# Attention scores of the first block: three rounded products of split queries and keys for one float32 product

## The chip, the cores and the metric

The program runs on one NeuronCore of a Trainium2 chip; the other cores are idle. The metric is the device time in microseconds (us) from the start to the end of one execution, and lower is better. Engines are named as in the profile: PE is TensorE's matrix multiplication, PEld its loading of the stationary operand (which can overlap PE), DVE is VectorE, ACT ScalarE, POOL GpSimd, SP the engine that issues DMAs here.

## What is computed

The reference runs two blocks on 512 tokens of width 1024. Only a part of the first block is touched, the differential attention of each of its two layers:

```python
qf = q.astype(f32).reshape(B, n_blk, Q_BLOCK, 2 * H, DIFF_DIM) * (DIFF_DIM ** -0.5)
...
s = jnp.einsum("bqmd,bkmd->bmqk", q_blk, kf)
dist = jnp.abs(qpos[:, None] - kpos[None, :]).astype(f32)
p = jax.nn.softmax(s - slopes[:, None, None] * dist, axis=-1)
p = p.reshape(B, H, 2, Q_BLOCK, S)
a = p[:, :, 0] - lam * p[:, :, 1]
return jnp.einsum("bhqk,bkhe->bqhe", a, vf)
```

H is 6 heads, each with two score maps m = 0 and 1 of width DIFF_DIM = 32. A block of queries is 128 tokens, and S is 512. The projections, a 31-tap depthwise convolution (computed beside the attention), the delta net, the MLP and the whole second block stay as they are.

## The kernel before

The first block is a loop of two turns (one for each layer); both turns run the same code, so every cost in the attention counts twice. Within a turn, each stage is a `phase` that starts and ends with a barrier of all engines: norm, projections, `diff_attention`, `delta_net`, norms and output projection, MLP. Inside a phase each engine follows its own list in the order in which the code is written, and waits on semaphores by hand-set counts.

`diff_attention` works through 24 units (j, t, h): j is one of three pairs of heads (a tile of 128 channels of q and k), t one of four blocks of 128 queries, h the head in the pair. A unit has two score maps, m = 0 and 1, in two PSUM banks of the four that `score_bank` hands out in turn. The two maps of a unit take their 32 channels from neighbouring lanes of the tile (lanes 0 to 31 and 32 to 63 for h = 0, 64 to 95 and 96 to 127 for h = 1).

- PE: after `scored(0)` and `scored(1)`, turn n is `scored(n + 2)`, `transposed(n)`, `apply(n - 1)` and, in every second turn, `turn_rows`. `scored` is the float32 product q times k for each m (L800, 32 rows of contraction, 512 columns), then one float32r product for each m that adds the distance term (L806). `transposed` turns the exponentials (L817), `apply` multiplies them with the values (L832, 16 instructions of 65 columns). `scored(n + 2)` waits until both exponentials of unit n are made, because it writes into their banks:

```python
if n >= 2:
    pe.wait_ge(exped, 2 * n - 2)
if (t, h) == (0, 0):
    pe.wait_ge(q_scaled, j + 1)
```

- ACT, unit n: `exponent(n)` (L742, two), `first_part(n - 2)` (L749), `take_rows` in every second unit from 5 on (L755), then the convolution's products `scale_taps` (L763), two after an even unit and three after an odd one. `exponent(n)` waits for the row minima of its unit. The queries are scaled in place by `scale_query` (L734), the first at the start and two more ahead of the units.
- DVE, unit n: `top(n)` (row minima, L865), `second_part(n - 3)` (L886), `take_turned(n - 1)` (L872), `invert_sums(n - 2)` (L877), which waits for the end of `apply(n - 2)` on PE. Ahead of the units DVE makes lambda, slopes, the rounded distances (L907), the values, the gated input of the convolution (L913) and its first tap (L917).
- POOL adds each scaled tap to y (L729, 60 in a turn).

Elsewhere (`linear`, L491 to L493) the kernel already makes a product of two float32 matrices as three float32r products: high times high, high times low, low times high, where high is the rounded value and low the rounded rest. `parts_of` allocates such a pair of tensors.

## Time and profile before

| | |
|---|---|
| median of 3 runs | 4620.15 us (4614.26 to 4620.54) |
| profiled execution, its own time | 4617.3 us |
| its span, first to last instruction | 4615.5 us |
| mean granted clock of TensorE | 0.891 of full speed |
| busy share of the span: PE, PEld, DVE, ACT, POOL | 88%, 73%, 36%, 29%, 4% |
| attention phase, first turn of the loop | from 187.5 to 307.6 us of the span |
| attention phase, second turn | from 1303.6 to 1423.7 us |

The busy share is an average over stages with different limits; what the attention waits for is read from its own stretches. A clock of 1.00 is 2.4 GHz, one of 0.50 is 1.2 GHz. The end of a matmul's record is modelled and includes latency: successive records overlap, so what one costs in a stream is the distance from its start to the next start, not its length.

### The profile page before, as it was taken

What the parts mean: (1) busy time and instruction counts of PE and PEld (TensorE: products, weight loads), DVE (VectorE), ACT (ScalarE), POOL (GpSimd) and SP (SyncE); (2) the same over time, 40 slices, a digit from 0 to 9 for tenths busy, and PEclk for the clock granted to TensorE, in tenths of its full rate; (3) what the DMA queues carried; (4) which work ended last, traced back from release to release, by engine and by line L of the source; (5) the groups of instructions that cost most, each with busy time, mean ns of one, the idle gap of its engine ahead of it and who ended that gap; (6) DMA issues with size and microseconds to landing.
All of it is one profiled execution on the core that took longest, in us unless ns stands there. A gap on an engine that the chain in (4) does not pass through costs nothing. (4 is left out here: it accounts for less than half of the span.)

```text
span 4615.5 us, 55382 instructions
## 1 busy us (share of the span) xinstructions
PE 4050.1 (88%) x21416; PEld 3361.9 (73%) x21416; DVE 1641.0 (36%) x2889; ACT 1327.6 (29%) x2306; POOL 194.7 (4%) x160
## 2 busy tenths in 40 slices
PE   7997888997998887999786777999878879999998
PEld 5777776775777775787465655787655569999998
DVE  2365435233246434423335434332245421111112
ACT  2464523231256433322132222222223311111111
POOL 0141000000033000000000000000000000000000
PEclk9997779998998878999897878999986689999999
DMA  3100012221200001222110001222220014545443
GB/s 116 41 1 1 0 37 82 86 96 45 99 5 1 0 0 55 91 91 91 55 59 1 0 18 64 80 99 76 89 91 0 18 49 182 191 161 189 167 152 130
DMA packets 51453, 324.51 MB, mean 70 GB/s; under 512 B 6528, under 2 KB 7424, under 8 KB 20352
## 3 DMA queue, kind: packets, MB, share of 16 engines
q1 hardware_dynamic: 51328, 322.85, 19.4%
q8 instruction: 78, 1.28, 0.1%
q14 instruction: 47, 0.39, 0.0%
HBM read 319.68 MB, written 2.10 MB: 70 GB/s over the span
## 5 line engine op out<-in xcount | busy, mean ns | idle before, releaser
L491 PE MATMUL bank<-high 128*128 128x512 f32 x2480 | 980.7, 395 | 116.0 <-DVE low L585 81.1
L492 PE MATMUL bank<-low,high 128*128 128x512 f32 x2480 | 976.4, 394 | 0.0
L493 PE MATMUL bank<-high,low 128*128 128x512 f32 x2480 | 975.4, 393 | 0.0
L491 PEld LDWEIGHTS bank<-high 128*128 128x128 f32 x2480 | 473.0, 191 | 224.2 <-issue 67.3
L492 PEld LDWEIGHTS bank<-low,high 128*128 128x128 f32 x2480 | 473.6, 191 | 98.5
L493 PEld LDWEIGHTS bank<-high,low 128*128 128x128 f32 x2480 | 472.7, 191 | 99.6
L549 DVE TENSOR_TENSOR low<-weight_ring,high 128x2048 fp32r<-128x2048 f32 (+1 forms) x144 | 319.2, 2218 | 553.1 <-ACT high L506 553.1
L2860 PE MATMUL bank<-chosen,glu_ring 128*128 128x176 f32 x2816 | 422.0, 313 | 0.0
L2860 PEld LDWEIGHTS bank<-chosen,glu_ring 128*128 128x128 f32 x2816 | 420.1, 190 | 0.0
L506 ACT ACTIVATE high<-weight_ring 128x2048 fp32r<-128x2048 f32 (+1 forms) x144 | 266.6, 1852 | 269.1 <-PE bank L493 230.2
L2871 PE MATMUL bank<-hidden,down_ring 128*128 128x176 f32 x1408 | 211.3, 313 | 0.0
L2871 PEld LDWEIGHTS bank<-hidden,down_ring 128*128 128x128 f32 x1408 | 210.4, 190 | 0.0
L1395 DVE TENSOR_TENSOR joint<-bank,level_masks 128x512 f32<-128x512 f32 x224 | 152.3, 689 | 129.4 <-PE bank L1410 129.4
L729 POOL TENSOR_TENSOR y<-y,scaled 128x512 f32<-128x512 f32 x120 | 149.6, 1274 | 1023.3 <-ACT scaled L763 1023.3
L2949 DVE TENSOR_TENSOR hidden<-silu,bank 128x176 f32<-128x176 f32 x88 | 29.7, 338 | 390.7 <-ACT silu L2917 390.7
L557 DVE TENSOR_TENSOR gated<-gated,bank 128x512 f32<-128x512 f32 x86 | 58.9, 685 | 287.5 <-ACT gated L513 158.2
L2917 ACT ACTIVATE silu<-bank 128x176 f32<-128x176 f32 x88 | 27.9, 317 | 445.5 <-PE bank L2860 445.5
L1417 PE MATMUL bank<-weight_ring,joint 128*128 128x128 f32 x1152 | 152.5, 278 | 0.0
L610 ACT ACTIVATE u<-bank 128x512 f32 (+1 forms) x84 | 50.3, 598 | 335.3 <-PE bank L493 335.3
L1410 PE MATMUL bank<-const_cols,weight_ring 128*128 128x128 f32 x672 | 108.3, 294 | 41.3 <-PEq L172 41.3
L1417 PEld LDWEIGHTS bank<-weight_ring,joint 128*128 128x128 f32 x1152 | 142.0, 195 | 0.0
L279 PE MATMUL bank<-squares,const_cols 128*128 128x512 f32 x144 | 82.6, 738 | 66.4 <-DVE squares L288 66.4
(465 smaller groups left out, 4972.9 us busy)
## 6 DMA issues: line engine op xcount, KB each, us to landing
glu_ring<-in_w_expert SPq DMA_DIRECT2D x88, 1024.0 KB, 4.8
weight_ring<-in_w_ff SPq DMA_DIRECT2D x64, 1024.0 KB, 5.2
down_ring<-in_w_expert_down SPq DMA_DIRECT2D x64, 704.0 KB, 5.1
weight_ring<-in_w_in SPq DMA_DIRECT2D x22, 1024.0 KB, 4.9
weight_ring<-in_w_ffe SPq DMA_DIRECT2D x22, 1024.0 KB, 4.8
weight_ring<-in_w_downe SPq DMA_DIRECT2D x16, 704.0 KB, 4.0
weight_ring<-in_w_ino SPq DMA_DIRECT2D x11, 1024.0 KB, 4.8
weight_ring<-in_w_ine SPq DMA_DIRECT2D x9, 1024.0 KB, 4.8
```

The source lines that it names most:

```text
L279: last = nc.tensor.matmul(total[:, :], CONST(mem.const, "ones"), squares[:, k, :], start=(k == 0), stop=(k == KD - 1))
L491: nc.tensor.matmul(mem.bank[b][:, :], whole, high[:, k, :], start=(k == 0), stop=False)
L492: nc.tensor.matmul(mem.bank[b][:, :], whole, low[:, k, :], start=False, stop=False)
L493: last = nc.tensor.matmul(mem.bank[b][:, :], rest, high[:, k, :], start=False, stop=(k == kt - 1))
L506: nc.scalar.activation(w_high[:, s, :], mem.ring[:, s, 0:size], ACT.Copy).then_inc(high_ready[s], 1)
L549: nc.vector.tensor_tensor(w_low[:, s, :], mem.ring[:, s, 0:size], w_high[:, s, :], ALU.subtract).then_inc(low_ready[s], 1)
L729: nc.gpsimd.tensor_tensor(y[:, c, :], y[:, c, :], scaled[:, n % CONV_SLOTS, :], ALU.add).then_inc(added, 1)
L1395: nc.vector.tensor_tensor(chunks(joint[:, n, :]), chunks(mem.bank[2 * n + 1][:, :]), mask, ALU.mult) \
L1410: last = nc.tensor.transpose(mem.bank[2 * n + 1][:, c], matrix[:, n, c], ident)
L1417: last = nc.tensor.matmul(mem.bank[2 * n][:, c], joint[:, n, c], matrix[:, n, c], start=True, stop=True)
L2860: last = nc.tensor.matmul(two(low[s])[:, half, :], glu_ring[:, s, at:at + P], chosen[:, k, :], start=(k == 0), stop=(k == KD - 1))
L2871: last = nc.tensor.matmul(two(high[m // 2])[:, m % 2, :], down_ring[:, s, k * P:(k + 1) * P], hidden[:, k, :], start=(k == 0), stop=(k == ...
```

## The change

The queries and keys of a pair of heads are split into a rounded value and a rounded rest, and the score product of each m becomes three float32r products (high q with high k, high q with low k, low q with high k), taken in turns over the two maps. ACT writes the two high parts (`round_pair`, which now also scales the queries), DVE the two rests (`rest_of_pair`). The first pair is split at the start of the phase, the next ones inside the loop, five or six units before they are used. To make room, `sig`, `probs`, `raw_dist`, `turned` and `scaled` move to memory that is free in this phase (the branch tensor `mem.h` and the weight ring); what is written and read there is the same.

```diff
-    with buffers(nc, padded=[P, CONV_T, SEQ + CONV_WIDTH - 1], sig=[P, CONV_T, SEQ], scaled=[P, CONV_SLOTS, SEQ],
-                 raw_dist=[P, DIST_COLS], prod=[P, 2, DIFF_DIM], dots=[P, 4], coef=[P, 1],
-                 values=[P, 2, TT, DIFF_HEADS, wide], probs=[P, 4, SEQ], turned=[P, 4, SEQ],
+    sig, probs = mem.h[:, 0:CONV_T, :], mem.h[:, 4:8, :]
+    raw_dist = mem.h[:, 2:4, :].rearrange("p k s -> p (k s)")[:, 0:DIST_COLS]
+    turned, scaled = [mem.ring[:, i, :].rearrange("p (n s) -> p n s", s=SEQ) for i in range(2)]
...
+            parts_of(nc, PAIRS1) as q_parts, parts_of(nc, PAIRS1) as k_parts, \
...
         @block.scalar
         def _(act):
-            def scale_query(j):
-                nc.scalar.activation(u[:, U_DQ + j, :], u[:, U_DQ + j, :], ACT.Copy, scale=-DIFF_DIM ** -0.5) \
-                    .then_inc(q_scaled, 1)
+            def round_pair(j):
+                nc.scalar.activation(q_parts[0][:, j, :], u[:, U_DQ + j, :], ACT.Copy, scale=-DIFF_DIM ** -0.5) \
+                    .then_inc(qk_high, 1)
+                nc.scalar.activation(k_parts[0][:, j, :], u[:, U_DK + j, :], ACT.Copy).then_inc(qk_high, 1)
...
-            scale_query(0)
+            round_pair(0)
...
-            for j in range(1, PAIRS1):
-                scale_query(j)
             act.wait_ge(padded_ready, CONV_T)
             for n in range(n_units):
+                if units[n][1:] == (TT - 2, 0) and units[n][0] + 1 < PAIRS1:
+                    round_pair(units[n][0] + 1)
                 exponent(n)
...
                 if (t, h) == (0, 0):
-                    pe.wait_ge(q_scaled, j + 1)
-                for m in range(2):
-                    lanes = slice(DIFF_DIM * (2 * h + m), DIFF_DIM * (2 * h + m + 1))
-                    nc.tensor.matmul(score_bank(2 * n + m)[:, :], u[lanes, U_DQ + j, t * P:(t + 1) * P],
-                                     u[lanes, U_DK + j, :], start=True, stop=False)
+                    pe.wait_ge(qk_split, 2 * j + 2)
+                for q_part, k_part in ((0, 0), (0, 1), (1, 0)):
+                    for m in range(2):
+                        lanes = slice(DIFF_DIM * (2 * h + m), DIFF_DIM * (2 * h + m + 1))
+                        nc.tensor.matmul(score_bank(2 * n + m)[:, :], q_parts[q_part][lanes, j, t * P:(t + 1) * P],
+                                         k_parts[k_part][lanes, j, :], start=(q_part == k_part), stop=False)
...
         def _(dve):
             steps = Steps(dve, dve_steps)
 
+            def rest_of_pair(j):
+                dve.wait_ge(qk_high, 2 * j + 1)
+                nc.vector.scalar_tensor_tensor(out=q_parts[1][:, j, :], in0=u[:, U_DQ + j, :], scalar=-DIFF_DIM ** -0.5,
+                                               in1=q_parts[0][:, j, :], op0=ALU.mult, op1=ALU.subtract) \
+                    .then_inc(qk_split, 1)
+                dve.wait_ge(qk_high, 2 * j + 2)
+                nc.vector.tensor_tensor(k_parts[1][:, j, :], u[:, U_DK + j, :], k_parts[0][:, j, :], ALU.subtract) \
+                    .then_inc(qk_split, 1)
...
+            rest_of_pair(0)
             for m in range(2):
                 steps.did(nc.vector.tensor_tensor(prod[:, m, :], lam_rows[:, 2 * m * DIFF_DIM:(2 * m + 1) * DIFF_DIM],
...
             for n in range(n_units):
+                if units[n][1:] == (TT - 2, 1) and units[n][0] + 1 < PAIRS1:
+                    rest_of_pair(units[n][0] + 1)
                 top(n)
```

In PE's list, units 0 and 1 and turn 0 of the attention stand as follows before (a row stands for a float32 product once, though it is two instructions on the engine):

```order
L800 MATMUL bank<-u 128x512 x2
L806 MATMUL bank<-dist,slopes 128x512 x2
L800 MATMUL bank<-u 128x512 x2
L806 MATMUL bank<-dist,slopes 128x512 x2
L800 MATMUL bank<-u 128x512 x2
L806 MATMUL bank<-dist,slopes 128x512 x2
L817 MATMUL bank<-const_cols,probs 128x128 x8
```

and now, with the score product at L805 and the distance term at L811 (`h_branch` is the new place of `probs`), unit 1 and turn 0:

```order
L805 MATMUL bank<-high 128x512 x2
L805 MATMUL bank<-low,high 128x512 x2
L805 MATMUL bank<-high,low 128x512 x2
L811 MATMUL bank<-dist,slopes 128x512 x2
L805 MATMUL bank<-high 128x512 x2
L805 MATMUL bank<-low,high 128x512 x2
L805 MATMUL bank<-high,low 128x512 x2
L811 MATMUL bank<-dist,slopes 128x512 x2
L822 MATMUL bank<-const_cols,h_branch 128x128 x8
```

A unit's score is six one-instruction products in place of two that are two instructions each; nothing else on PE moved.

In ACT's list, this stands around `exponent(4)` before (the exponentials of units 2, 3 and 4, with the taps behind each):

```order
L742 ACTIVATE probs<-bank,tops 128x512 x2
L749 ACTIVATE part<-bank,inv 128x64
L763 ACTIVATE scaled<-padded,vec 128x512 x2
L742 ACTIVATE probs<-bank,tops 128x512 x2
L749 ACTIVATE part<-bank,inv 128x64
L763 ACTIVATE scaled<-padded,vec 128x512 x3
L742 ACTIVATE probs<-bank,tops 128x512 x2
```

and now, from the exponentials of unit 3 on:

```order
L746 ACTIVATE h_branch<-bank,tops 128x512 x2
L753 ACTIVATE part<-bank,inv 128x64
L767 ACTIVATE weight_ring<-padded,vec 128x512 x3
L737 ACTIVATE high<-u 128x512
L739 ACTIVATE high<-u 128x512
L746 ACTIVATE h_branch<-bank,tops 128x512 x2
```

The two roundings stand between the taps of unit 3 and the exponentials of unit 4; the same is so ahead of unit 12.

In DVE's list, `top(5)` followed the reciprocal of unit 2 at once; now the two rests stand between them, and likewise ahead of `top(13)`:

```order
L891 RECIPROCAL inv<-bank 128x2
L869 SCALAR_TENSOR_TENSOR low<-u,high 128x512
L873 TENSOR_TENSOR low<-u,high 128x512
L879 TENSOR_REDUCE tops<-bank 128x1 x2
L900 SCALAR_TENSOR_TENSOR rows<-bank,inv,part 128x64
```

## Rows read from the trace of the kernel before

**Rows 1.** Windows: length, busy us of PE, PEld, DVE, ACT, POOL; PEclk; DMA.
```profile
188.65:209.13 20.48, 16.47 (x47) 8.42 (x43) 11.04 (x25) 12.81 (x19) 6.17 (x5) 0.50 0.06 22
209.13:308.10 98.97, 96.57 (x687) 76.30 (x686) 61.98 (x134) 67.39 (x133) 68.61 (x55) 1.00 0.00 1
...
245.00:260.00 15.00, 15.00 (x101) 11.13 (x101) 10.04 (x22) 10.19 (x21) 9.95 (x9) 1.00 0.01 2
```
**Rows 2.** Waits from 215 to 300 us: who waited for whom, total, times, longest.
```profile
ACT part L749 <- DVE inv L877: 26.2, 20, 1.6
DVE inv L877 <- PE bank L832: 15.5, 19, 0.8
```
**Rows 3.** Timeline of one steady turn on PE: start, length, engine, line.
```profile
227.72 1.13 PE L800 MATMUL bank<-u 32*128 32x512 f32 x4
...
228.78 0.30 PEld L806 LDWEIGHTS bank<-dist,slopes 128*128 128x128 f32 x2 [0.76 <-issue]
...
232.16 1.13 PE L800 MATMUL bank<-u 32*128 32x512 f32 x4
```
**Rows 4.** Narrow windows in that turn: its four score instructions, and their loads.
```profile
227.72 0.70 PE L800 MATMUL bank<-u 32*128 32x512 f32 x2
...
228.26 0.59 PE L800 MATMUL bank<-u 32*128 32x512 f32 x2
...
227.83 0.19 PEld L800 LDWEIGHTS bank<-u 32*128 32x128 f32 x2
```
**Rows 5.** Timeline of float32r products in a stream, at full and at half clock.
```profile
150.12 0.39 PE L492 MATMUL bank<-low,high 128*128 128x512 f32 x1
150.35 0.39 PE L493 MATMUL bank<-high,low 128*128 128x512 f32 x1
...
66.57 0.63 PE L492 MATMUL bank<-low,high 128*128 128x512 f32 x1
66.99 0.63 PE L493 MATMUL bank<-high,low 128*128 128x512 f32 x1
```
**Rows 6.** By line: the query scaling; then timeline at the phase's start.
```profile
L734 ACT ACTIVATE u<-u x6: 612/614/629, 187.5 to 1310.6; 128x512 f32<-128x512 f32 x6
...
192.16 0.16 DVE L902 TENSOR_TENSOR coef<-dots 128x1 f32<-128x1 f32 x1 [2.75 <-ACT dots L770]
194.03 1.13 ACT L734 ACTIVATE u<-u 128x512 f32<-128x512 f32 x2
196.96 1.26 ACT L742 ACTIVATE probs<-bank,tops 128x512 f32<-128x512 f32 x2 [1.80 <-DVE tops L865]
198.28 2.08 PE L800 MATMUL bank<-u 32*128 32x512 f32 x4 [0.79 <-ACT probs L742]
```
**Rows 7.** Timeline where ACT makes the exponentials of units 4 and 12.
```profile
217.00 1.25 ACT L742 ACTIVATE probs<-bank,tops 128x512 f32<-128x512 f32 x2
218.96 0.70 PE L800 MATMUL bank<-u 32*128 32x512 f32 x2
...
252.08 1.26 ACT L742 ACTIVATE probs<-bank,tops 128x512 f32<-128x512 f32 x2
254.01 1.13 PE L800 MATMUL bank<-u 32*128 32x512 f32 x4
```
**Rows 8.** Timeline of DVE, ACT and POOL around unit 13.
```profile
254.21 1.26 DVE L865 TENSOR_REDUCE tops<-bank 128x1 f32<-128x512 f32 x2
255.76 1.25 ACT L742 ACTIVATE probs<-bank,tops 128x512 f32<-128x512 f32 x2
251.04 3.74 POOL L729 TENSOR_TENSOR y<-y,scaled 128x512 f32<-128x512 f32 x3 [1.98 <-ACT scaled L763]
258.45 1.13 PE L800 MATMUL bank<-u 32*128 32x512 f32 x4
```
**Rows 9.** DVE operations with two SBUF inputs, by line: shortest, median, longest ns.
```profile
L585 DVE TENSOR_TENSOR low<-h_branch,high x8: 682/683/691, 63.7 to 67.9; 128x512 fp32r<-128x512 f32 x8
L298 DVE SCALAR_TENSOR_TENSOR h_branch<-x_res,vec,scale x8: 746/746/752, 30.0 to 34.6; 128x512 f32<-128x512 f32 x8
```

More of the change, by code:

```diff
@@ L691, in diff_attention @@
     taps = [(i, c) for i in range(1, CONV_WIDTH) for c in range(CONV_T)]
-    with buffers(nc, padded=[P, CONV_T, SEQ + CONV_WIDTH - 1], sig=[P, CONV_T, SEQ], scaled=[P, CONV_SLOTS, SEQ],
-                 raw_dist=[P, DIST_COLS], prod=[P, 2, DIFF_DIM], dots=[P, 4], coef=[P, 1],
-                 values=[P, 2, TT, DIFF_HEADS, wide], probs=[P, 4, SEQ], turned=[P, 4, SEQ],
+    sig, probs = mem.h[:, 0:CONV_T, :], mem.h[:, 4:8, :]
+    raw_dist = mem.h[:, 2:4, :].rearrange("p k s -> p (k s)")[:, 0:DIST_COLS]
+    turned, scaled = [mem.ring[:, i, :].rearrange("p (n s) -> p n s", s=SEQ) for i in range(2)]
+    with buffers(nc, padded=[P, CONV_T, SEQ + CONV_WIDTH - 1], prod=[P, 2, DIFF_DIM], dots=[P, 4], coef=[P, 1],
+                 values=[P, 2, TT, DIFF_HEADS, wide],
                  tops=[P, 2 * n_units], inv=[P, n_units, 2], part=[P, 2, HEAD], rows=[P, 2, P]) as (
-            padded, sig, scaled, raw_dist, prod, dots, coef, values, probs, turned, tops, inv, part, rows), \
+            padded, prod, dots, coef, values, tops, inv, part, rows), \
+            parts_of(nc, PAIRS1) as q_parts, parts_of(nc, PAIRS1) as k_parts, \
             nc.sbuf_tensor(f"dist_{nc.next_id()}", [P, DIST_COLS], F32R) as dist, \
             nc.sbuf_tensor(f"slopes_{nc.next_id()}", [P, DIFF_HEADS, P], F32R) as slopes, phase(
-            nc, "loaded", "q_scaled", "gate_ready", "dots_ready", "exps_ready", "coef_ready", "bias_ready",
+            nc, "loaded", "qk_high", "qk_split", "gate_ready", "dots_ready", "exps_ready", "coef_ready", "bias_ready",
             "values_ready", "values_scaled", "padded_ready", "conv_begun", "scaled_ready", "added", "score", "topped",
@@ L702, in diff_attention @@
             "rows_taken", "dve_steps") as (
-            block, loaded, q_scaled, gate_ready, dots_ready, exps_ready, coef_ready, bias_ready,
+            block, loaded, qk_high, qk_split, gate_ready, dots_ready, exps_ready, coef_ready, bias_ready,
             values_ready, values_scaled, padded_ready, conv_begun, scaled_ready, added, score, topped,
```

## The prediction, on record before the changed kernel ran

> **What bounds the kernel now.** I read the page for the stages, then the windows of the attention phase, its waits, and its timeline. The page says that PE is busy 88% of the span, which tells nothing of this phase; the windows do: from 245 to 260 us PE is busy for all 15.00 us, while DVE has 10.04, ACT 10.19 and POOL 9.95 [rows 1]. The waits have only one sort of entry: the reciprocal on DVE waits for PE, and ACT's `part` waits for that reciprocal [rows 2]. Nobody makes PE wait in the steady turns. A turn lasts 4.44 us (227.72 to 232.16, the two score starts [rows 3]). So what PE saves in a turn is saved in the phase, as long as ACT and DVE keep up. The exception is the start: PE's third score, at 198.28, waits for the first exponentials on ACT, and these for DVE's row minima [rows 6]. The granted clock is 0.50 from 188.65 to 209.13 us and 1.00 behind it [rows 1].
>
> **What the score costs now.** From the first score instruction to the distance term is 228.78 - 227.72 = 1.06 us for both maps [rows 3]. The narrow windows show how: two instructions start at 227.72, two at 228.26, and the second pair's loads at 227.83, while the first pair streams [rows 4]. The two maps use different lanes and run side by side. The first pair takes 0.54 us, the second 0.52 to the distance term. I read 0.43 of each as two streams of 512 columns (a float32r instruction, one such stream, has starts 0.427 apart at half clock, 66.57 to 66.99 [rows 5], so a stream at full clock is 0.213), and the other 0.11 and 0.09 as fixed: the first load, which nothing covers (the second record, 0.59, is shorter than the first, 0.70, by just that), and the change from 32-row to 128-row products, ahead of which PEld is idle [rows 3, 4].
>
> **What it will cost.** Six float32r instructions, three pairs in a row. In a stream such products start 0.23 apart (150.12, 150.35; 0.227 over several [rows 5]). No row shows one with 32 rows. If they pair as float32 does: 3 x 0.227 = 0.68 for 0.853 of streams, and both fixed parts stay. That saves 0.17 us in a turn. Bounds: 3 x 0.213 = 0.64 (saves 0.21) if the 0.014 of overhead hides under the partner, and 6 x 0.227 = 1.36 (loses 0.51) if nothing pairs. I take 0.17, since row groups of 32 lanes and loads are the same as in [rows 4], and only the number type differs. At half clock the saving is 1.71 - 3 x 0.427 = 0.43.
>
> How often: units 0 and 1 lie ahead of the wait at 198.28 and save nothing. Units 2 and 3 are scored at half clock: 0.86. Units 4 to 23 are 20 at full clock: 3.5 us.
>
> **The start.** ACT has one more operation ahead of the sigmoids. Two such copies in a row take 1.13, a single one 0.61 [rows 6], so one adds 0.52. DVE begins with two rests that it must wait for, but it stands idle 2.75 us ahead of L902 anyway, waiting for ACT [rows 6]; two operations of such sizes take 0.75 and 0.68 [rows 9], and with the wait for the high parts they end about 2.1 us later than DVE began before. That fits into the idle time; without this cover they would cost those 2.1 instead of 0.52. Lambda, distances, the first minima and so PE's third score come 0.52 late, at half clock. The two queries that ACT no longer scales at 194.03 were covered by its wait of 1.80 [rows 6] and give nothing. Of 0.86 saved at half clock, 0.86 - 0.52 = 0.34 is left, which is worth half once the clock has risen: 0.15 us.
>
> **The roundings inside the loop.** `round_pair` stands ahead of `exponent(4)` and `exponent(12)`, behind three taps. Before, those exponentials run from 217.00 to 218.25 and from 252.08 to 253.34, and PE, which needs them for the score two units on, starts at 218.96 and 254.01 [rows 7]. Slack: 0.71 and 0.67, of which 0.06 is what the semaphore takes (198.22, the end of the first exponentials, to 198.28 [rows 6]). Two copies add 2 x 0.52 = 1.04, and PE wants the result 0.17 earlier than before. PE stalls 1.04 - (0.65 - 0.17) = 0.56, and 1.04 - (0.61 - 0.17) = 0.60: 1.16 us in a phase. Behind it in ACT's list stand `part` and the taps, which POOL waits for; POOL has a third of its time free.
>
> `rest_of_pair` delays DVE ahead of `top(5)` and `top(13)` by 0.66 + 0.60, some 1.3 us (the distance of such operations in a row: 30.0 to 34.6 and 63.7 to 67.9 us over seven steps [rows 9]). For unit 13, minima start at 254.21, the exponentials at 255.76, held by ACT's own taps, and end at 257.01; PE needs them at 258.45 [rows 8]. With 1.3 more the minima end at 256.8, the last exponential at 257.5. Slack is left, and the rests cost nothing. `take_turned` on DVE starts later by less than PE's stall. The rests themselves are wanted two turns on.
>
> **The sum.** One phase: -0.15 - 3.5 + 1.16 = -2.5 us; two turns of the loop: -5.0. Moved buffers: nothing, the one DMA is the same. Of the profiled time of 4617.3 us that leaves 4612.3. The median of the runs lies 2.9 higher than the profiled run, 4620.15, so I expect **4615.2 us**, 0.11% less.
>
> **A rule on shared ports.** POOL's additions, 1.25 us each, run while the rests would: three from 251.04 to 254.78 [rows 8]. No DVE operation in this phase has two SBUF inputs beside POOL, so no row has its price. The Trainium skill (SBUF — State Buffer, Who interferes with whom) says that a DVE instruction with two SBUF inputs and a GpSimd instruction that reads SBUF block each other for a whole instruction. What blocking as a mechanism would cost here follows from [rows 8]: the first rest waits for 254.78, 0.57 late, the second for one more addition, 1.25. The minima then end at 258.6, the exponentials at 259.3, against PE's need at 258.45 + 0.6 - 0.17 = 258.9: up to 0.4 us more stall at each of four places, 1.7 in all, or 4616.9. I give this a chance of 0.3, inside the main case below, which it hardly moves. By that rule, rests in the loop would have records of over 1 us.
>
> **Rivals.**
> - *Loads no longer hide* (0.10). A stream is now 0.213 long, not 0.43, and must cover the next load to the same lanes, 0.11. For: each load of the first pair is exposed. Against: the second pair's load starts at 227.83, inside the first pair's stream on the same lanes [rows 4]. If each pair shows its load: 3 x (0.213 + 0.107) = 0.96 + 0.09 = 1.05, no saving in a turn. Nothing is saved, the late start costs 0.26 (0.52 at half clock) and the stalls are 2 x 0.17 shorter, 0.8: 2 x 1.06 = +2, or 4622. The same skill (TensorE: Matmul & The Clock Gate, Part 3, The mechanism) says that a load overlaps a matmul only when the row group differs, which would be this case; the 227.83 load contradicts it, so the chance is small.
> - *No pairing of float32r: slower* (0.13). PE runs them one behind the other, from one map's to the other's. Each unit loses 0.51 at full clock (20 units, 10.2 us) and 0.85 at half clock (1.7 for two, with the late start 2.2, worth 1.1). ACT's stalls vanish, since its slack grows to 1.16. Sum 2 x 11.3 = +22.6: 4643. It decides as soon as fewer than about half of the pairs overlap. For: no row with 32 rows in float32r. Against: the maps and banks are what pairs float32.
> - *Clock* (0.04). Less streaming on PE could keep the half clock longer at the phase's start: each us costs half, 20 us more in both phases would be +20. Against: PE is as gapless as before from 198.8 us on.
> - *Better than the sum* (0.10). Overhead hides (0.21 in a turn) and the copies squeeze into ACT's slack: 2 x (4.3 + 0.15) = -8.9, with luck in the later, clock-dependent stages beyond -9: 4610.
>
> **How the numbers follow.** The main case has 0.63, from -9 to +0.5 us. A difference under 0.2% (9.2 us) is about what a measurement can't tell from none; the three runs before spread over 6.3 us. Same: main, hidden loads, and part of the better case: 0.71. Slower: no pairing and clock: 0.17. Faster: the rest of the better case and the low end of the main one, with luck in later stages: 0.12. The range for eight in ten leaves out the case without pairing and half of the outermost: 4608 to 4625.
>
> **What would show it.** L805 with 288 records, in three pairs of starts 0.23 apart, and 0.88 us from first score start to distance term (1.06 before). The turn of 4.44 becomes 4.27. PE waiting for ACT's exponentials twice in a phase, near 219.4 and 254, by 0.6. The first distance term at 193.6, the third score at 198.8. I am wrong if the six records start one after the other, if the stalls are over 1 us, or if the clock rises later than some 21 us after its fall.

## The result: 5.7 us longer, outside the range

| | before | after |
|---|---|---|
| median of 22 runs each, us | 4620.34 | 4626.03 |
| all runs, us | 4606.82 to 4633.55 | 4621.54 to 4637.98 |
| ratio of the two, 95% interval | | 1.0017, 1.0009 to 1.0025 |
| profiled execution, span, us | 4615.5 | 4624.1 |

Forecast were 4615.2 us and a range of 4608 to 4625. That is 0.12%, under the 0.2% that the prediction took for what a measurement can't tell from none, but it is 5.7 us more where 5.0 less was forecast. (The ratio here and below isn't the quotient of the two medians; where the two disagree, the text says so.)

**Inside the attention nearly every step came as forecast.** By line, the new score instructions (columns: shortest, median, longest ns; first and last start), and the remainders on DVE:
```profile
L805 PE MATMUL bank<-high x96: 489/494/792, 188.3 to 1416.0; 32*128 32x512 f32 x96
L805 PE MATMUL bank<-low,high x96: 382/392/627, 188.9 to 1416.4; 32*128 32x512 f32 x96
L805 PE MATMUL bank<-high,low x96: 383/392/627, 189.3 to 1416.6; 32*128 32x512 f32 x96
...
L869 DVE SCALAR_TENSOR_TENSOR low<-u,high x6: 693/1240/1291, 187.0 to 1377.6; 128x512 fp32r<-128x512 f32 x6
...
L873 DVE TENSOR_TENSOR low<-u,high x6: 677/679/685, 187.6 to 1378.8; 128x512 fp32r<-128x512 f32 x6
```
PE's timeline where the scores of units 5 and 6 are made (start, us, line; answers to [rows 3, 7]):
```profile
212.87 0.50 PE L805 MATMUL bank<-high 32*128 32x512 f32 x2
213.21 0.39 PE L805 MATMUL bank<-low,high 32*128 32x512 f32 x2
213.44 0.40 PE L805 MATMUL bank<-high,low 32*128 32x512 f32 x2
213.76 0.73 PE L811 MATMUL bank<-dist,slopes 128*128 128x512 f32 x2
214.33 1.04 PE L822 MATMUL bank<-const_cols,h_branch 128*128 128x128 f32 x8
215.21 1.90 PE L837 MATMUL bank<-values,weight_ring 128*128 128x65 f32 x16
217.58 0.50 PE L805 MATMUL bank<-high 32*128 32x512 f32 x2 [0.47 <-ACT h_branch L746]
```
Two maps still run side by side (x2 in one row), a score takes 213.76 - 212.87 = 0.89 us (1.06 in [rows 3]), and the turn that ends at 217.58 holds a stall that is new (the 0.47 in brackets). The waits from 205 to 300 us count two of them (total, times, longest; [rows 2] had none):
```profile
PEld bank L805 <- ACT h_branch L746: 1.3, 2, 0.7
PE bank L805 <- ACT h_branch L746: 1.0, 2, 0.5
```
DVE, POOL and ACT beside that stall:
```profile
217.23 1.25 DVE L869 SCALAR_TENSOR_TENSOR low<-u,high 128x512 fp32r<-128x512 f32 x1
218.40 0.68 DVE L873 TENSOR_TENSOR low<-u,high 128x512 fp32r<-128x512 f32 x1
...
214.19 3.74 POOL L732 TENSOR_TENSOR y<-y,weight_ring 128x512 f32<-128x512 f32 x3 [1.67 <-ACT weight_ring L767]
218.42 3.03 POOL L732 TENSOR_TENSOR y<-y,weight_ring 128x512 f32<-128x512 f32 x2 [0.49 <-ACT weight_ring L767]
...
215.24 0.62 ACT L737 ACTIVATE high<-u 128x512 fp32r<-128x512 f32 x1
215.76 0.62 ACT L739 ACTIVATE high<-u 128x512 fp32r<-128x512 f32 x1
216.28 1.25 ACT L746 ACTIVATE h_branch<-bank,tops 128x512 f32<-128x512 f32 x2
```
The two roundings push the exponentials of unit 4 to 216.28, and PE gets them 0.5 us late.

**What the attention saved, the stage behind it gave back.** Windows of before: the attention, `delta_inputs` behind it, and the three `delta_scan` of the first pass (length; busy us of PE, PEld, DVE, ACT, POOL; PEclk):
```profile
187.50:308.40 120.90, 113.48 (x732) 85.02 (x732) 74.08 (x164) 81.31 (x153) 74.79 (x60) 0.91 0.02 5
308.40:347.80 39.40, 30.98 (x216) 30.79 (x216) 24.04 (x49) 24.60 (x44) 0.00 (x0) 0.74 0.00 1
...
406.90:434.40 27.50, 23.10 (x176) 17.47 (x176) 4.87 (x23) 4.39 (x12) 0.00 (x0) 0.88 0.00 1
492.50:526.90 34.40, 30.25 (x176) 21.32 (x176) 4.87 (x23) 4.39 (x12) 0.00 (x0) 0.60 0.00 0
584.90:616.20 31.30, 27.50 (x176) 18.57 (x176) 4.87 (x23) 4.39 (x12) 0.00 (x0) 0.66 0.00 0
```
The same of after:
```profile
186.30:304.70 118.40, 108.99 (x780) 90.15 (x780) 78.70 (x170) 82.99 (x156) 75.90 (x60) 0.91 0.02 5
304.70:346.70 42.00, 33.57 (x216) 33.38 (x216) 24.04 (x49) 24.71 (x44) 0.00 (x0) 0.72 0.00 1
...
405.50:440.00 34.50, 30.28 (x176) 21.33 (x176) 4.87 (x23) 4.42 (x13) 0.00 (x0) 0.60 0.01 1
497.90:529.60 31.70, 27.51 (x176) 18.57 (x176) 4.88 (x23) 4.40 (x13) 0.00 (x0) 0.66 0.00 0
588.70:624.80 36.10, 32.26 (x176) 23.07 (x176) 4.87 (x23) 4.39 (x12) 0.00 (x0) 0.56 0.00 0
```
The attention is 2.5 us shorter, as forecast, and `delta_inputs` 2.6 us longer with the same 216 products: its PE is busy 2.6 us longer at a lower mean clock. From the phase's first ACT operation to the first of `delta_prepare`, the stage after `delta_inputs`, it is 160.27 us before and 160.38 after (second pass 160.33 and 160.79). The scans, in which the kernels' code is the same, differ by +7.0, -2.7 and +4.8, and each time the longer one has the lower clock. In these two profiles, the whole difference of 8.6 us is already there when the second pass starts (1303.6 and 1312.2 us), and the three scans alone make 9.1.

The two stages ahead of the scans can be taken apart further. Stretches around `delta_inputs` of before, then of after:
```profile
308.12:328.60 20.48, 13.87 (x65) 13.88 (x66) 17.24 (x35) 13.21 (x23) 0.00 (x0) 0.50 0.00 1
328.60:347.80 19.20, 17.11 (x153) 16.92 (x152) 6.80 (x14) 11.39 (x21) 0.00 (x0) 1.00 0.00 1
...
306.43:326.91 20.48, 15.88 (x74) 15.88 (x75) 15.63 (x30) 12.24 (x23) 0.00 (x0) 0.50 0.00 1
330.32:333.74 3.42, 3.42 (x18) 3.42 (x18) 2.10 (x6) 1.84 (x3) 0.00 (x0) 0.50 0.01 2
```
Before, the clock falls 0.3 us ahead of the stage, stays at 1.2 GHz for 20.5 us and is at 2.4 GHz from there to the stage's end. After, it falls 1.7 us into the stage, so that more of the products lie under the 20.5 us, and it falls once more later, for 3.4 us. (In the second pass of after it falls 1.5 us ahead of the stage, for 23.9 us, and again 25.8 us into it for 3.4.) In the first pass PE is busy at half clock for 13.87 us before and for 15.88 + 3.42 = 19.30 after. Work at half clock takes twice its time, so half of the difference, 2.7 us, is an estimate of the loss; measured are 2.6.

So two things had to be found out: whether the clock or the splitting makes `delta_inputs` longer, and where the scatter of some 20 us between executions comes from, in which 5 us must be seen.

### The profile page after: what moved, and what is told of

It is laid out like the page before. It is cut to its first block and busy times, and to the rows that moved or that the text cites. A ratio compares the mean times of both kernels' runs of the same rounds, so it can differ in the third digit from the quotient of the medians.

```text
span 4624.1 us, 55592 instructions
## 1 busy us (share of the span) xinstructions
PE 4055.5 (88%) x21512; PEld 3383.8 (73%) x21512; DVE 1650.3 (36%) x2901; ACT 1331.5 (29%) x2312; POOL 197.0 (4%) x160
## 5 line engine op out<-in xcount | busy, mean ns | idle before, releaser
L732 POOL TENSOR_TENSOR y<-y,weight_ring 128x512 f32<-128x512 f32 x120 | 151.8, 1291 | 1020.0 <-ACT weight_ring L767 1020.0
```

Source lines behind the costliest of these rows:

```text
L732: nc.gpsimd.tensor_tensor(y[:, c, :], y[:, c, :], scaled[:, n % CONV_SLOTS, :], ALU.add).then_inc(added, 1)
```

## The experiments

Theory A: TensorE's granted clock steps between 1.2 and 2.4 GHz, and what a stage takes depends on where a stretch at half clock lies on its products; an attention that ends sooner moves that stretch. Theory B, the rival: the splitting itself costs the stages behind it. All runs, with ratios to before on the same chip; the last two columns are read from the profiled execution, first pass / second pass: us from the phase's first ACT operation to the first product of `delta_inputs`, and to the first operation of `delta_prepare`.

| run | median us (lowest to highest, n) | ratio, 95% | to first product | to `delta_prepare` |
|---|---|---|---|---|
| before | | | 127.2 / 127.2 | 160.3 / 160.3 |
| after | 4626.0 (4621.5-4638.0, 22) | 1.0017, .0009-.0025 | 124.7 / 125.0 | 160.4 / 160.8 |
| e1, after, +10 pairs | 4631.9 (4619.9-4644.0, 5) | 1.0038, .0025-.0051 | 127.3 / 127.0 | 160.2 / 159.8 |
| e2, after, +5 pairs | 4641.5 (4623.0-4655.2, 6) | 1.0055, .0034-.0076 | 125.8 / 125.8 | 159.3 / 159.3 |
| e3, after, +15 pairs | 4634.3 (4629.7-4649.8, 6) | 1.0043, .0030-.0057 | 128.2 / 128.2 | 163.8 / 163.8 |
| e4, before, shortened | 4623.0 (4612.1-4639.4, 12) | 1.0017, .0004-.0029 | 124.7 / 124.7 | 160.6 / 160.6 |
| e5, after, filled | 4622.8 (4602.3-4639.4, 12) | 0.9994, 0.9978-1.0010 | 124.6 / 122.9 | 157.5 / 154.2 |
| e6, before, filled | 4611.9 (4601.3-4640.6, 12) | 0.9977, .9960-.9994 | 124.8 / 124.8 | 152.9 / 157.7 |
| e7, moved, filled | 4609.2 (4600.6-4625.7, 9) | 0.9967, .9952-.9981 | 121.9 / 121.9 | 150.0 / 150.0 |
| e8, moved, filled, scans | 4582.6 (4580.6-4586.9, 4) | 0.9909, .9894-.9924 | 121.9 / 121.9 | 153.2 / 153.3 |
| e9, before, scans | 4593.4 (4588.1-4604.4, 6) | 0.9938, .9924-.9952 | 126.9 / 127.3 | 159.8 / 160.4 |
| e10, after, scans | 4602.7 (4586.3-4604.6, 6) | 0.9946, .9930-.9962 | 125.1 / 124.6 | 160.8 / 160.2 |
| e11, before, filled, scans | 4587.8 (4585.9-4588.5, 5) | 0.9924, .9911-.9936 | 124.8 / 124.8 | 152.9 / 157.7 |
| e12, after, filled, scans | 4584.9 (4579.6-4585.5, 5) | 0.9917, .9904-.9929 | 122.9 / 122.9 | 154.2 / 154.2 |
| e13, moved, trimmed | 4580.2 (4572.5-4587.0, 5) | 0.9918, .9904-.9931 | 119.6 / 119.6 | 154.3 / 149.4 |
| e14, before, trimmed | 4575.0 (4573.9-4582.3, 5) | 0.9913, .9899-.9926 | 122.5 / 122.5 | 157.1 / 153.9 |
| e15, after, trimmed | 4576.9 (4572.1-4577.8, 4) | 0.9909, .9894-.9924 | 122.3 / 122.2 | 156.9 / 156.8 |
| e16, before, tail only | 4586.6 (4584.0-4599.8, 6) | 0.9928, .9911-.9945 | 127.6 / 127.7 | 160.6 / 160.7 |
| e17, after, tail only | 4580.7 (4577.3-4590.6, 6) | 0.9915, .9899-.9931 | 125.1 / 125.0 | 156.5 / 156.4 |
| e18, moved, tail only | 4579.7 (4572.9-4586.1, 6) | 0.9909, .9893-.9925 | 124.1 / 124.1 | 157.1 / 157.1 |

### 1. Length alone: e1 to e4

e1 to e3 add superfluous high-high pairs (their result is overwritten) to the changed kernel's last units (e1 one for n >= 14, e2 one for n >= 19, e3 e1's and one more for n >= 19):
```diff
-                for q_part, k_part in ((0, 0), (0, 1), (1, 0)):
+                extra = 1 if n >= 14 else 0
+                for p, (q_part, k_part) in enumerate(((0, 0),) * (extra + 1) + ((0, 1), (1, 0))):
...
-                                         k_parts[k_part][lanes, j, :], start=(q_part == k_part), stop=False)
+                                         k_parts[k_part][lanes, j, :], start=(q_part == k_part), stop=(p < extra))
```
e4 takes the kernel before and shortens it by as much as the change did, by leaving out the distance term of the second map from unit 13 on (its output is therefore not the reference's):
```diff
+                    alone = m == 1 and n >= 13
...
-                                     u[lanes, U_DK + j, :], start=True, stop=False)
+                                     u[lanes, U_DK + j, :], start=True, stop=alone)
...
+                    if m == 1 and n >= 13:
+                        continue
```
Expected of e1:

> The changed kernel with one superfluous pair of high-high products (overwritten by the next) in each of the units 14 to 23: 10 pairs of 0.23 us, so the attention is as long as in the kernel before (some 120 us) with PE busy. Theory A (what the attention saves is lost because the next stage, delta_inputs, meets the half-clock stretch at another place): delta_inputs falls back from 42.0 to about 39.4 us in both turns, and the time to that of before, ratio 1.000 +- 0.001, although 4.6 us of work were added. Theory B (the splitting itself costs somewhere, whatever its length): delta_inputs stays at 42.0 and the ratio is 1.0017 + 4.6/4620 = 1.0027.

Of e2:

> The same with 5 superfluous pairs in units 19 to 23: the attention is 1.1 us longer than in the changed kernel, 2.3 us in both turns. Theory B: ratio 1.0022. Theory A gives no straight line: delta_inputs somewhere between 39.4 and 42.5, and a ratio between 1.000 and 1.002, which must not be the mean of its neighbours.

Of e3:

> The same with 15 superfluous pairs: 3.4 us longer than the changed kernel, 6.8 us in both turns. Theory B: ratio 1.0032. Theory A: if the clock falls at the same place in the next stage as in the changed kernel, delta_inputs is 42.0 again and the ratio also about 1.003; if at the place of before, 39.4 and 1.001.

Of e4:

> The kernel before, with float32 scores and no splitting, but shorter: the distance term of the second score map is left out in units 13 to 23 (11 products of 0.23 us), so its result is not the reference's. Attention 117.6 us in place of 120.1. Theory A: delta_inputs grows from 39.4 to 42.0 here too, and the ratio is 1.000 to 1.002, not below 1, though 5 us of work are gone. Theory B: delta_inputs stays at 39.4 and the ratio is 1 - 5/4620 = 0.9989.

Windows of the attention and `delta_inputs` in e1:
```profile
186.90:307.80 120.90, 111.56 (x800) 92.26 (x800) 78.71 (x170) 82.88 (x156) 75.87 (x60) 0.91 0.02 5
307.80:347.10 39.30, 30.89 (x216) 30.70 (x216) 24.03 (x49) 24.59 (x43) 0.00 (x0) 0.75 0.01 1
```
The same in e2:
```profile
185.80:305.30 119.50, 109.42 (x790) 90.67 (x790) 78.73 (x170) 82.99 (x156) 75.97 (x60) 0.93 0.02 5
305.30:345.10 39.80, 31.34 (x216) 31.15 (x216) 24.04 (x49) 24.63 (x44) 0.00 (x0) 0.74 0.00 1
```
In e3:
```profile
186.20:308.10 121.90, 112.48 (x810) 92.94 (x810) 78.69 (x170) 82.92 (x156) 75.89 (x60) 0.92 0.02 5
308.10:350.10 42.00, 33.54 (x216) 33.35 (x216) 24.04 (x49) 24.75 (x44) 0.00 (x0) 0.72 0.01 1
```
In e4:
```profile
187.70:306.10 118.40, 110.92 (x721) 83.20 (x721) 74.10 (x164) 81.37 (x154) 74.85 (x60) 0.91 0.02 5
306.10:348.30 42.20, 33.83 (x216) 33.63 (x216) 24.04 (x49) 24.70 (x43) 0.00 (x0) 0.69 0.01 1
```
With the attention lengthened by 2.5 us and the splitting kept (e1), `delta_inputs` is back at 39.3; with the kernel before shortened by 2.5 us and no splitting (e4), it is 42.2, and the whole is as much longer as the changed kernel: 1.0017 in both. That refutes theory B for this stage. It is no straight line either: 42.0 at 118.4, 39.8 at 119.5, 39.3 at 120.9, 42.0 again at 121.9. The second stretch at half clock tells the two groups apart: after, e3, e4 and e10, whose stage takes 42 us, have one of 3.4 us some 25 us into it, in both passes; before, e1, e2 and e9, at 39 to 40 us, have none. But the totals don't follow: by the medians e1, e2 and e3 are 12.9, 22.5 and 15.3 us above before on the same chip. The ratio of e1 is over theory A's (1.000), and theory B's 1.0027 lies in its interval; that of e2 is over both (A up to 1.002, B 1.0022); e3's interval just reaches the 1.003 of both. So it is the stage's own length that speaks against theory B here, and e4, not these totals. The profiled execution of e1 is the fastest of its five (4619.9), so its trace can't show why the median is high. The spreads of 24 and 32 us of e1 and e2 pointed at the scans.

### 2. The clock held up: e5 to e8

e5 to e8 give PE products nobody reads where it waits:
```diff
+def fill(nc, mem, bank, count):
+    for _ in range(count):
+        nc.tensor.matmul(mem.bank[bank][:, 256:256 + P], CONST(mem.const, "ones"), CONST(mem.const, "ident"),
+                         start=True, stop=True)
...
+            fill(nc, mem, 5, 8)
             scored(0)
             scored(1)
+            fill(nc, mem, 5, 6)
...
+            fill(nc, mem, 3, 28)
             pe.wait_ge(g_ready, 1)
```
e7 and e8 also move the roundings apart (ACT; the remainders on DVE likewise), and e8 fills each `delta_scan`:
```diff
-                if units[n][1:] == (TT - 2, 0) and units[n][0] + 1 < PAIRS1:
-                    round_pair(units[n][0] + 1)
+                if units[n][1:] == (TT - 3, 0) and units[n][0] + 1 < PAIRS1:
+                    round_query(units[n][0] + 1)
+                if units[n][1:] == (TT - 2, 0) and units[n][0] + 1 < PAIRS1:
+                    round_key(units[n][0] + 1)
...
+            fill(nc, mem, 4, 8)
             pe.wait_ge(solved_taken, 4)
```

Expected of e5 to e8, in this order:

> The changed kernel with work on TensorE that nobody reads (ones times the identity, 128 x 128) where it waits around the attention: 8 products before the first scores, 10 before the first distance term, 6 after the second unit's scores, 6 ahead of each of the last row turns and 6 behind them, and 28 before the first product of delta_inputs. The output is unchanged. Theory A (what the attention saves is given back because TensorE's granted clock steps fall elsewhere in the stage behind it): with no stretch at half clock there, delta_inputs takes the same time as in the kernel before with the same filling, some 36 us or less in both, and this kernel is 4 to 6 us shorter than that one in the two turns taken together. Theory B (the splitting itself makes the following stage longer): delta_inputs stays 2.5 us longer than in the kernel before with the same filling, and their times agree within 2 us. If the clock falls all the same, neither is tested.

> The kernel before with the same filling on TensorE at the same places. The output is unchanged. Theory A: delta_inputs without a stretch at half clock, 36 us or less against 39.4, attention a little under its 120.9; in all 4605 to 4615 us. Theory B says nothing of this kernel by itself: it is what the changed kernel with filling is compared with, and by B the two agree within 2 us.

> The changed kernel with the same filling, and the two roundings of a pair on ScalarE apart, the queries' ahead of unit 2 (10) and the keys' ahead of unit 4 (12), with the two remainders on VectorE apart likewise. The output is unchanged. Forecast from the stalls of the changed kernel: each pair of roundings together (1.24 us) made the scores of units 6 and 14 0.53 and 0.60 us late; one alone (0.62 us) fits the slack of some 0.65 us that this leaves per turn, so both stalls go: the attention 1.0 to 1.2 us shorter than with filling alone, and 2 to 2.4 us off the whole if the clock stays up behind it (theory A); nothing off the whole if the following stages give it back.

> The one before it with 8 more superfluous products in each delta_scan, while TensorE waits for the copies of the solved values. The output is unchanged. Theory A in its wider form (the scatter of 20 us between executions is delta_scan of 27.6 or 34.5 us, by whether TensorE's clock falls some 13.6 us into it): most of the six scans of the first block's two passes take 27.6 us, and the whole is 10 to 30 us shorter with less scatter. If the scans stay at 31 to 34.5 us, the fall isn't due to that wait, and the time is that of the one before within 5 us.

The half-clock stretch of 20 us at the attention's start is gone in all four. In `delta_inputs` the clock fell all the same, for 13.7 and 10.2 us in e5's two passes and for 3.4 and 13.7 in e6's, so for that stage these runs test neither theory, as e5's expectation says for this case. Up to the first product of `delta_inputs` the change is then worth 124.8 - 122.9 = 1.9 us (e5's second pass; in the first the clock dropped once more), and apart from its stalls 2.9 (e7). The totals of e5 and e6 say the opposite, +11 us, with spreads of 37 and 39 us: that expectation was missed, and runs that scatter so can't carry it. e8 shows where most of the scatter comes from. Its three scans of the first pass:
```profile
397.60:425.90 28.30, 25.04 (x192) 19.41 (x192) 4.88 (x23) 4.39 (x12) 0.00 (x0) 0.86 0.01 2
483.60:508.70 25.10, 21.86 (x192) 16.43 (x192) 4.89 (x23) 4.41 (x13) 0.00 (x0) 0.96 0.00 0
567.60:598.70 31.10, 28.21 (x192) 22.35 (x192) 4.88 (x23) 4.40 (x13) 0.00 (x0) 0.78 0.00 0
```
Each has sixteen more records of PE, some of them on the path (28.3 against the 27.5 of before's best), and yet the median is 26.6 us under e7's and 46.5 under that of before, with a spread of 6 us (four runs) against e7's 25 (nine). The expectation had most scans at 27.6 us; instead they take 28.3, 25.1 and 31.1, and half-clock time is left in each. What the filling brought is that they are the same each time: in the profiles of all runs from e8 on, both passes have these three lengths to 0.4 us (e13's second pass in another order), while the same scans without it took anything from 24.0 to 38.0 us.

### 3. The change with calmer scans: e9 to e12

e9 is before and e10 after with the scans' filling alone, e11 and e12 have the filling of e5 as well. Expected of e9 to e12:

> The kernel before with 8 products that nobody reads (ones times the identity, 128 x 128) in each delta_scan, ahead of its wait for the copies of the solved values, and no other filling. The output is unchanged. Where the last run but one of this study found delta_scan to be the source of the scatter (the same 8 products, with other edits beside them, took the spread from 20 to 30 us down to 6 and the median down by 1.0%), this kernel has a spread of at most 12 us and lies at 4575 to 4600 us. It is the ruler for the next one.

> The changed kernel with the same 8 products in each delta_scan and no other filling. The output is unchanged. Theory A (what the attention saves is given back in delta_inputs by where the clock steps fall): attention 118.5 and delta_inputs 42 against 120.9 and 39.4, and a total within 2 us of that of the kernel before with the same products. The prediction's sum, had it been right for the whole kernel: 5 us less. Theory B (the splitting itself costs): 4 to 10 us more, as between the two kernels without the products.

> The kernel before with the products in delta_scan and with the filling around the attention (24 products at its start, 30 at its end, 28 before the first product of delta_inputs). The output is unchanged. The clock stays up in the attention, which ends some 4 us earlier than without filling, and its last products are some 2.7 us late behind too much filling; 3 to 12 us less in all than with the products in delta_scan alone. It is the ruler for the next one.

> The changed kernel with the products in delta_scan and the filling around the attention. The output is unchanged. Theory A: from the first operation of the attention to the first product of delta_inputs it is 1.9 us shorter per pass than the kernel before with the same filling (seen in profiles without the products in delta_scan: 122.8 against 124.8), and with the scatter gone the whole is shorter too, by 3 to 6 us for two passes, since no half-clock stretch behind the attention takes it back. Against the run with the roundings moved apart (4582.6) it is 1.5 to 3 us longer. Theory B: no shorter than the kernel before with the same filling.

e11 and e12 go as theory A says, at the low end: 2.9 us between the medians, and each of e12's five runs is under each of e11's on the same chip; 1.9 us a pass up to the first product. `delta_inputs` still isn't equal: in the first pass e11 reaches `delta_prepare` 1.3 us sooner than e12 (152.9 and 154.2), in the second 3.5 us later, as its clock fell for 3.4 and 13.7 us against 10.2 in both of e12's. Without the attention's filling, e9 and e10 reach `delta_prepare` level over the two passes (320.2 and 321.0 us together) and come out of the first block alike (`token_major`'s third start is at 2239.8 and 2239.3 us), so nothing of what the attention saved is left there. Yet e10's median is 9.3 above e9's where 2 were expected (by the ratios 0.08%, under 4 us), and their spreads, 16 and 18 us, are over the 12 that e9's expectation allowed. Of the 6 us between their profiles, 6.7 arise in `sparse_attention`, 1200 us on (222.2 and 228.9 us), which neither kernel fills. That the change makes that stage fall the bad way more often isn't shown.

### 4. Less filling, and a dip of the change's own: e13 to e15

As e8, e11 and e12, but 3, 3 and 2 products at the attention's end, 20 ahead of `delta_inputs`, and 3 in each `rwkv_scan`, a stage of the second block. Expected:

> The changed kernel with the roundings apart, the products in delta_scan, and the filling around the attention cut so that it no longer delays anything: 3, 3 and 2 products at the attention's end in place of 6, 6 and 6, and 20 in place of 28 ahead of delta_inputs; 3 more in each rwkv_scan. The output is unchanged. The first product of delta_inputs came 17.8 us after the attention's last exponential with the longer filling and 15.1 without; here 15.1 to 15.5 if the clock stays up, so up to 2.5 us per pass less. 4572 to 4582 us, and 4 to 8 us below the kernel before with the same additions.

> The kernel before with the same products in delta_scan, in rwkv_scan and around the attention. The output is unchanged. 4580 to 4588 us; from the first operation of the attention to the first product of delta_inputs 122 us (127.2 without any filling). It is the ruler for the other two.

> The changed kernel with the same products in delta_scan, in rwkv_scan and around the attention, the roundings where the change put them. The output is unchanged. Theory A: below the kernel before with the same additions by 1.9 us per pass in the attention, 2 to 5 us in all (2.9 between the medians of the pair with the longer filling), and 1.5 to 3 us above the run with the roundings apart.

The expected order didn't come: by the medians e15 is 1.9 above e14 and e13 5.1, while by the ratios e15 is a hair below e14 (0.9909 and 0.9913), so between those two nothing is decided; e14 is also 5 us faster than its expectation began. For e15 the trace shows a loss inside the attention. PE's timeline at the first stall:
```profile
212.48 0.50 PE L811 MATMUL bank<-high 32*128 32x512 f32 x2 [0.47 <-ACT h_branch L752]
...
213.37 1.07 PE L818 MATMUL bank<-dist,slopes 128*128 128x512 f32 x2
214.24 1.91 PE L829 MATMUL bank<-const_cols,h_branch 128*128 128x128 f32 x8
```
and the two windows behind it:
```profile
212.50:213.55 1.05, 1.05 (x7) 0.64 (x8) 1.05 (x2) 1.05 (x3) 0.55 (x2) 1.00 0.00 0
213.56:216.98 3.42, 3.42 (x16) 3.12 (x15) 3.18 (x6) 1.58 (x3) 2.77 (x2) 0.50 0.01 2
```
e14 at the same place:
```profile
213.00:217.00 4.00, 4.00 (x29) 3.11 (x30) 2.83 (x6) 2.69 (x5) 3.12 (x3) 1.00 0.01 2
```
PE came back from the stall that the roundings made at 212.48, was busy without a gap, and 1.1 us later its clock fell for 3.4 us: eight transposes took 1.91 us instead of 1.04. It did so in both passes, and not in e13, where the stall is gone: its score instructions no longer stand in its list of waits, and from the first to the 24th unit's exponentials it took 94.1 us against 96.7 in e15 and 97.5 in e14. e12 separates the dip from the stall: its attention is the same as e15's up to the last turns, has the same two stalls and no dip, and takes 95.1 us in both passes. So the dip cost 1.7 us, and the two stalls together 1.0 (e12 against e13). Such a dip is rare: the nine profiles with the roundings in pairs have 36 such stalls, and three of them have one, the two here and one in e5's first pass. All three began 1.1 us after PE had resumed, which ties them to the stall; all three are in kernels whose attention's start is filled. Why the other 33 had none isn't shown. e13's total is high all the same: three of its four `rwkv_scan` took the longer 22 us where e14 and e15 have one, and `sparse_attention` 228.9 against 222.4 in e14.

### 5. Only the stage behind: e16 to e18

As e14, e15 and e13 without the filling at the attention's start. Expected:

> The kernel before with the filling at the attention's end (3, 3, 2), 20 products ahead of delta_inputs, 8 in each delta_scan and 3 in each rwkv_scan, and none at the attention's start. The output is unchanged. The attention begins with its 20.5 us at half clock as in the kernel before; delta_inputs takes what it took with this filling, 36.4 us in the first pass. It is the ruler for the other two; 4580 to 4590 us.

> The changed kernel with the same filling. The output is unchanged. Theory A (only where the clock steps fall behind the attention takes back what it saved): the attention is shorter by 2.5 us per pass as without filling, delta_inputs the same in both kernels within 0.5 us in the first pass, so delta_prepare begins 2.0 us earlier relative to the end of the stage ahead, and the whole is 1 to 6 us below the kernel before with the same filling. Theory B (splitting lengthens the stage behind it): delta_inputs 2.6 us longer than in that kernel, in all no less.

> The same with the roundings apart (the queries' ahead of unit 2, the keys' ahead of unit 4, remainders likewise). The output is unchanged. Both stalls of 0.5 to 0.6 us behind the roundings go, and the attention is another 1.1 us shorter per pass than in the run before this; 1 to 3 us less in all, if no stage behind it takes it back.

Windows of attention and `delta_inputs` of e16 (before):
```profile
187.30:308.60 121.30, 115.18 (x748) 86.80 (x749) 74.06 (x164) 81.44 (x154) 74.76 (x60) 0.92 0.02 5
308.60:347.90 39.30, 35.60 (x256) 35.22 (x256) 23.95 (x49) 24.95 (x44) 0.00 (x0) 0.83 0.00 1
```
Of e17 (after):
```profile
186.10:304.90 118.80, 110.60 (x796) 91.94 (x796) 78.69 (x170) 83.00 (x156) 75.94 (x60) 0.91 0.02 5
304.90:342.60 37.70, 33.97 (x256) 33.62 (x256) 23.95 (x49) 24.96 (x44) 0.00 (x0) 0.86 0.01 1
```
Of e18 (after, roundings apart):
```profile
185.90:303.70 117.80, 110.61 (x796) 91.96 (x797) 79.13 (x170) 83.36 (x157) 74.94 (x60) 0.91 0.02 5
303.70:343.00 39.30, 35.60 (x256) 35.24 (x256) 23.95 (x49) 24.95 (x44) 0.00 (x0) 0.83 0.01 1
```
Now the change keeps what it saves: 2.5 us a pass in the attention, and 1.6 more in `delta_inputs`, again by the clock (down for 13.7 us of that stage in e16 and 10.2 in e17). The expectations had `delta_inputs` equal in the two within 0.5 us, and at 36.4 us in e16, where it took 39.3: both were missed. The whole is 5.9 us below e16 between the medians (of 36 pairings of their runs, e17's is the shorter in 32), where the prediction's sum was 5.0. The nearness of these two is partly luck: of the 8.2 us that the two stages gained over two passes, 3.2 are the clock's in `delta_inputs`, and the spreads are 16 and 13 us. With the roundings apart another 1.0 us a pass goes in the attention, `delta_inputs` takes 1.6 back, and the whole comes out 1.0 lower, which the spreads can't tell from nothing.

All of e8 and e11 to e18 are 0.7 to 0.9% faster than before and after; the lowest medians, e14 and e15, differ by less than their spreads. So what these experiments point to as faster is the filling, with or without the change.

## Why the prediction was wrong

- **The score**: right. Three pairs overlap, 0.88 us forecast, 0.89 measured; turns of 4.27 were forecast, PE's turn of 4.44 became 4.27 (221.85 - 217.58), and two turns now take 3.51 + 4.93 us by the starts of ACT's exponentials, 4.22 each (3.67 + 5.09, 4.38 each, before).
- **The start**: right. PE's third score starts 11.28 us behind the phase's first operation (197.60 - 186.32) against 10.75 before (198.28 - 187.53), 0.53 later where 0.52 was forecast; DVE's remainders were covered.
- **The roundings**: right, 0.56 and 0.60 forecast, 0.53 and 0.60 measured (turns of 4.71 and 4.76 against 4.18 and 4.16). That the clock can dip behind such a stall (e15) was not seen. The roundings and remainders stand four and three units ahead of the next pair's first unit, not the five or six that the text on the change gives; nothing waited for it.
- **Shared ports**: half right. In the loop the remainder with two SBUF inputs took 1.24 to 1.29 us where it began during an addition of POOL, 0.69 at the phase's start with POOL idle. In the rows above it begins at 217.23, POOL's running additions end at 214.19 + 3.74 = 217.93, and it ends 0.55 us behind them; at the other three places it is 0.54 or 0.55. So the record of over 1 us came as the rule of the Trainium skill (SBUF — State Buffer, Who interferes with whom) has it. The forecast let the second remainder wait for one more addition; here it was the other way: it began at 218.40, 0.02 ahead of POOL's next addition, took only 0.68, and POOL's two additions took 3.03 us instead of 2.50. Whoever began first went on, the other waited. No further stall of PE came of it; [rows 8] had enough slack.
- **The phase**: right, 2.5 us less (2.2 to 2.5 up to the first product of `delta_inputs`).
- **"Of the profiled time of 4617.3 us that leaves 4612.3"**: this step failed. It carried the phase's saving over to the kernel, as if all behind it moved up unchanged. `delta_inputs`, for which the sum had no term, took it back, 2.6 us in the first pass: its PE worked 19.3 us at half clock instead of 13.9. e4 shows that it isn't the change: with the same shortening and no splitting the loss is the same. e16 and e17 show the reverse: with PE kept busy behind the attention and in the scans the saving arrives.
- **The clock rival** looked at the phase's own start alone and at +20 us. There the stretch stayed at 20.5 us. It gave a chance of 0.04 to the mechanism that decided the outcome, in a place where it did nothing; the clock moved things behind the phase, where the prediction had read no row.
- **The range** held the unknowns of the attention but only -9 to +0.5 for the rest, while `delta_scan` alone takes 27.5 or 34.4 us for the same work in one execution of before.

**Open** is why the median came out 5.7 us above and not merely even. Even is what the attention and `delta_inputs` show. The record says by what the executions differ, though not why: over the 72 executions of before that ran beside the experiments (two that took 8 and 14 ms left out), the time falls by 3.9 us for each 0.001 of mean granted clock (correlation -0.92). Their mean clock is 0.8892, that of the 22 executions of the changed kernel 0.8873. At equal clock the changed kernel isn't the longer one: at 0.888 the medians are 4626.9 (ten of before) and 4624.6 (ten of after). So the excess goes with more time at half clock. `delta_inputs` explains a part of that; in the two profiles the rest lies in the three `delta_scan` of the first pass, which differ between executions of one kernel as well. Whether the change shifts how often they fall the bad way would take many profiles of each kernel, and wasn't measured; nor is it on record whether all these executions ran on the same chips.

## What to carry to other kernels

Where a kernel's profile shows half-clock stretches at the joints between stages, a saving in one stage is a change of position for all behind it: read the windows of the next stage before carrying it into the sum, and put the difference between the same stage's instances (27.5 and 34.4 us here) into the range. Before comparing variants a few us apart, calm the stages that scatter; eight idle products at one wait of the scans took the spread from 25 us (e7) to 6 (e8), and without filling around the attention still left 16 and 18 (e9, e10). Part of that narrowing is the smaller number of runs. And a stall added on PE costs more than its length if the clock dips behind it, as it did in three cases of 36: spread inserted work over turns, one operation to each.

## What was not expected of the hardware

- Products nobody reads paid: 8 in each `delta_scan` made the kernel before 0.62% faster (e9), with those around the attention 0.76 to 0.87% (e11, e14), though each took some 0.22 us, and in e11 those at the attention's end and ahead of the next stage together delayed the first product of `delta_inputs` by 2.7 us (17.8 instead of 15.1 us behind the last exponentials).
- A stall of 0.47 us in an otherwise gapless PE was followed, 1.1 us after PE had resumed, by 3.4 us at 1.2 GHz, in both passes of e15, though not in e12, which has the same stalls.
- PE's work at half clock priced the loss: 5.4 us more of it in `delta_inputs` of after than of before cost 2.6 us; the same estimate gives 3.0 for e4 (measured 2.8).
- A DVE operation of 0.69 us with two SBUF inputs took 1.25 when it began during an addition of POOL, and one of 0.68 that began 0.02 us ahead of an addition took no longer while the addition took 0.5 more. In e13 and e18, with one remainder to a turn, POOL's next addition took at most 1.32 us.
